# Three waits for the state-space mixer's end moved three steps later, with half-weight steps for the memory rows' sums

## The reference, cut to what matters

```python
h = rms_norm(x, norm_mix_g)
u = h @ w_in
y_ssd  = ssd_mixer(u[..., :SSD_IN], ...)     # ends in a grouped RMS norm
y_rwkv = rwkv7_mixer(u[..., SSD_IN:], ...)   # first uf = u + (u_prev - u) * mu
...
m = rms_norm(mem, norm_mem_g)                # 256 memory rows x 2048
k, v = m @ wk, m @ wv
```

## Time and profile before

| | before |
|---|---|
| median of three runs | 3058.83 us (3057.3 to 3061.13) |
| profiled execution | 3055.73 us, of which the span from first to last instruction is 3053.9 us |
| TensorE busy | 2975.5 us, 97% of the span |
| VectorE / ScalarE / GpSimd busy | 2074.0 / 1412.6 / 241.1 us |
| mean granted TensorE clock | 0.994 |
| chunks 33 to 39 of `in_rwkv` on TensorE | 294.29 to 316.17 us |
| longest TensorE idle time of the stage | 3.11 us |

### The profile page before, as it was taken

The page is one execution under the profiler, slowest core; times in us unless marked ns, Lnnn a source line. Parts: engine busy times, 40 slices in busy tenths (PEclk is TensorE's granted clock), DMA queues, the critical chain, the costliest instruction groups (busy, mean ns, idle before and its releaser), DMA issues.

```text
span 3053.9 us, 52430 instructions
## 1 busy us (share of the span) xinstructions
PE 2975.5 (97%) x21994; PEld 2632.0 (86%) x21994; DVE 2074.0 (68%) x2869; ACT 1412.6 (46%) x1977; POOL 241.1 (8%) x201
## 2 busy tenths in 40 slices
PE   8999999999999999999999999999989999999998
PEld 7899988887888888888888899888878888888887
DVE  6486864645656787888888985555677666666666
ACT  5343542534444563544445454444336445444453
POOL 1100321110100200000000310010010000000002
PEclk9999999999999999999999999999999999999999
DMA  7555566766645669888888877755345565665664
GB/s 250 166 167 156 158 222 206 225 196 227 209 138 159 214 198 280 274 277 277 273 279 277 271 234 225 221 151 170 109 131 162 183 187 178 202 187 184 180 186 132
DMA packets 527580, 619.94 MB, mean 203 GB/s; under 512 B 19450, under 2 KB 443541, under 8 KB 525984
## 3 DMA queue, kind: packets, MB, share of 16 engines
q1 hardware_dynamic: 518672, 586.31, 62.2%
q0 software_dynamic: 3344, 23.78, 2.2%
q10 hardware_dynamic: 5328, 6.49, 0.6%
HBM read 608.12 MB, written 8.39 MB: 202 GB/s over the span
## 4 chain that ended last, share of the span: by engine, by line
PE 90%; DVE 5%; issue 3%; ACT 1%; DMA 0%; POOL 0%; ACTq 0%; POOLq 0%; DVEq 0%; SPq 0%
PE psum L605 37%; PE psum L606 19%; PE psum L574 6%; PE psum L576 6%; PE psum L577 6%; PE psum L639 2%; PE psum L641 2%; PE psum L642 2%; DVE wlo L531 1%; PE psum L1851 1%; PE psum L706 1%; DVE cacc L1118 1%; PE psum L2563 1%; PE psum L2082 0%; PE psum L2304 0%
## 5 line engine op out<-in xcount | busy, mean ns | idle before, releaser
L524 ACT ACTIVATE whi<-wraw 128x1024 fp32r<-128x1024 f32 (+1 forms) x948 | 978.6, 1034 | 1001.2 <-PE psum L606 692.7
L531 DVE TENSOR_TENSOR wlo<-wraw,whi 128x1024 fp32r<-128x1024 f32 (+1 forms) x948 | 1151.2, 1230 | 244.6 <-ACT whi L524 244.1
L605 PE MATMUL psum<-g,whi 128*128 128x512 f32 x2816 | 996.1, 396 | 11.0 <-DVE g L2603 4.1
L605 PE MATMUL psum<-h,whi 128*128 128x512 f32 x2240 | 790.7, 395 | 2.3 <-DVE wlo L531 1.3
L606 PE MATMUL psum<-g,wlo 128*128 128x256 f32 x2816 | 787.0, 279 | 0.0
L605 PEld LDWEIGHTS psum<-g,whi 128*128 128x128 f32 x2816 | 529.0, 188 | 139.9 <-issue 8.4
L606 PE MATMUL psum<-h,wlo 128*128 128x256 f32 x2240 | 634.1, 283 | 0.0
L606 PEld LDWEIGHTS psum<-g,wlo 128*128 128x128 f32 x2816 | 529.2, 188 | 0.5
L605 PEld LDWEIGHTS psum<-h,whi 128*128 128x128 f32 x2240 | 421.4, 188 | 100.3 <-DVE wlo L531 1.6
L606 PEld LDWEIGHTS psum<-h,wlo 128*128 128x128 f32 x2240 | 421.9, 188 | 0.1
L574 PE MATMUL psum<-h,whi 128*128 128x256 f32 x1040 | 304.0, 292 | 22.0 <-DVE h L958 13.7
(11 more groups left out here) (488 smaller groups left out, 3191.3 us busy)
## 6 DMA issues: line engine op xcount, KB each, us to landing
wraw<-in_ffn_w SPq DMA_DIRECT2D x256, 512.0 KB, 4.9
wraw<-in_w_in SPq DMA_DIRECT2D x204, 512.0 KB, 3.7
wraw<-in_ada_w SPq DMA_DIRECT2D x192, 512.0 KB, 4.2
wraw<-in_ffn_w_up SPq DMA_DIRECT2D x160, 512.0 KB, 3.6
wraw<-in_w_out SPq DMA_DIRECT2D x64, 512.0 KB, 3.7
wraw<-in_ffn_w_down SPq DMA_DIRECT2D x64, 512.0 KB, 4.5
wraw<-in_xattn_wk SPq DMA_DIRECT2D x32, 512.0 KB, 4.6
wraw<-in_xattn_wv SPq DMA_DIRECT2D x32, 512.0 KB, 4.9
```

Source lines behind the costliest of these rows:

```text
L524: e.activation(high(i), raw(i), ACT.Copy).then_inc(*hi.up(i))
L531: e.tensor_tensor(low(i), raw(i), high(i).bitcast(F32), SUB).then_inc(*lo.up(i))
L605: e.matmul(both_of(g, j), w_hi[:, kk, s:s + 128], X[:, k, :], start=k == 0, stop=False, skip_group_check=True)
```

## The change

On all three engines three empty steps, `idle(3)`, come between the mixer's own steps and the wait for its end. The steps of the memory rows' sums weigh 0.5 in place of 1: on TensorE and VectorE the 7 empty ones and the one with the work, on ScalarE all 8. Nothing is added or removed in what is computed, and GpSimd's program is as before.

```diff
-            side = Side(ssd_p(e), then(psum_of_ssd_read, e), sums_p(e, mem, TM2, True), idle(12))
+            side = Side(ssd_p(e), idle(3), then(psum_of_ssd_read, e), sums_p(e, mem, TM2, True, 0.5), idle(12))
...
-            side = Side(ssd_v(e), then(ssd.ended, e), sums_v(e, mem, RS2, RC2[:, :]), mixing_v(e, 0, 12))
+            side = Side(ssd_v(e), idle(3), then(ssd.ended, e), sums_v(e, mem, RS2, RC2[:, :], 0.5), mixing_v(e, 0, 12))
...
-            side = Side(ssd_a(e), then(ssd.ended, e), then(mem_landed, e), sums_a(e, mem, MX, TM2, RS2, RC2[:, :]), idle(12))
+            side = Side(ssd_a(e), idle(3), then(ssd.ended, e), then(mem_landed, e), sums_a(e, mem, MX, TM2, RS2, RC2[:, :], 0.5), idle(12))
```

## The result

The changed kernel takes 3063.53 us (median of 20 runs, 3058.5 to 3066.43). The kernel before, run beside it, takes 3057.54 us (20 runs). The ratio is 1.0020, with a 95% interval of 1.0014 to 1.0026: about 6.0 us slower, at the edge of what was forecast as no measurable change (2.3 us). The profiled execution took 3064.98 us, its span 3063.2 us.

The account below looks back on a forecast made before the run. TensorE bounds, VectorE second: minus 3.1 of hole and 1.7 of clock, plus 6.2 of new wait and 1.7 of clock, net 2.2, rounded to plus 2.3 us: 3061.1 us as a median, range 3056.5 to 3066.6.

Parts of the forecast that it names:

- The removed wait: TensorE's wait for the mixer's end at 291: 3.11 us of hole and 1.7 us of low clock go, gaining 4.8.
- Where the steps fall: TensorE waits for the mixer after chunk 35 instead of 32, and makes the memory sums after chunk 38 instead of 39.
- the new hole: TensorE ahead of the memory sums: it waits for GpSimd's last add from 308.3 to 314.5, 6.2 us.
- The chain of squares and adds: ScalarE's squares and GpSimd's adds alternate strictly ahead of the sums: 11.0 us taken, 12.5 the other measurement.
- VectorE as the second bound: Without clock loss, VectorE's low part for chunk 47 at 341.3 bounds: plus 1.1 us, 3059.9; chance 0.15.
- The clock term: TensorE behind the new 6.2 us wait: low clock costs 1.7 us, at least nothing, at most 3.4.
- The sum: TensorE reaches chunk 47 at 342.4 against 340.24, a net of 2.2 us later, kept to the end.
- Range and chances: Whole-kernel time 3056.5 to 3066.6 us; chances 0.87 for same, 0.08 for slower, 0.05 for faster.
- the worst case summed up: Squares and adds taking 12.5 us and a clock loss of 3.4 us: plus 5.5 us, 3064.3.
- The 0.08 for slower: Chance of slower by more than 0.2%: the old hole not being this wait (3065.9), or very slow adds.
- no case but one: The one case: adds of up to 3.31 us and a long low-clock stretch on TensorE, 3064.3 us; chance 0.15.

Follow-up runs that it names:

- tensor_wait_late: Kernel before, with only TensorE's wait for the mixer's end three steps later and the memory sums kept behind chunk 39: 3052.78 us, ratio 0.9988.
- before_filled: Kernel before, with 7 extra unused matmuls on TensorE ahead of its wait for the mixer's end: ratio 0.9987, stage 1.7 us shorter.
- filled: Changed kernel, with 14 extra unused matmuls on TensorE ahead of its wait for GpSimd's last add: 3057.28 us, ratio to before 0.9998.
- sums_39: Changed kernel, with sums' steps of 0.65 on TensorE and VectorE (ScalarE keeps 0.5), so the sums come behind chunk 39: ratio to before 1.0003.
- half_only: Kernel before, with half steps for the sums on three engines, mixer waits unmoved, idle(3) behind VectorE's reciprocal: 3066.27 us, ratio 1.0026.

## Why the prediction was right in kind and short in size

- **The removed wait, 4.8 us:** right. `tensor_wait_late` shows 4.8, `before_filled` 1.7 for the clock alone.
- **Where the steps fall, and the new hole:** right. TensorE waits 6.04 us (6.2 forecast), the sums start at 314.57 (314.5).
- **The chain of squares and adds:** 10.6 us, a little under both bounds (11.0 and 12.5; 11.0 was taken), with adds of 2.34 to 2.48 us. Before, an add took 3.31 us beside VectorE's low parts. After, VectorE stood still for 17.01 us ahead of its reciprocal, and the two adds that began in that time took 2.34 us each. The Trainium skill (GPSIMD Engine Reference, 1. Specifications) says that GpSimd shares its SBUF interfaces with VectorE and contends with VectorE instructions that have two SBUF inputs, as L531 has. The trace agrees.
- **VectorE as the second bound at +1.1 us:** right where it came to bind, in `filled`. In the changed kernel the reciprocal was forecast for 318.6 and started at 322.26, because the sums ahead of it ran at the lower clock.
- **The clock term failed.** "For a hole of 6.2 us I take 1.7 us again; below nothing, above 3.4." It was 5.9: the sums took 7.0 us instead of 3.4, and chunk 39 took 326.8 - 321.6 = 5.2 instead of 2.85. The upper bound of 3.4 was itself too low. I took both numbers from stretches in which other matmuls followed the hole. What followed this one, L932 and L936, was in the trace, but I priced it by its duration at the full clock alone.
- **The sum again:** 2.2 + (5.9 - 1.7) = 6.4 us at TensorE; the stage grew by 5.9. Of the difference, 0.5 us, the start of the sums gives 0.2: the mixer's last L1204 starts 0.28 us later in this profile than in before's, and counted from there the sums start at 314.3, not at 314.5. The rest is tenths in the length of the sums and behind chunk 47.
- **Range and chances:** 3063.53 lies in the range, and in part by luck. The loss of 6.0 us is more than the worst case summed up, plus 5.5. The three runs of before that the forecast started from had a median 1.3 us above that of all 20, so the time is 2.4 us off the forecast of 3061.1 where the change is 3.7 us off. The kernel is slower by just 0.2%, and that is told from no change here: the interval reaches 1.8 us to each side. The 0.08 for slower was too little, because no case but one priced a longer low stretch.

## What to carry to other kernels

When a wait is moved to after its event, move the consumers behind it too: count, on every engine, in which iteration each step lands, and add up the chain across engines that must fit between. Here the three later steps alone were worth 4.9 us, and the half steps on top of them cost 10.8. A hole in TensorE's work costs its length plus the low clock behind it, and that second part depends on what runs next: behind the hole of 6.0 us it was 2.1 us with a full chunk first and 5.9 us with the sums first. If the hole can't be avoided, unused wide matmuls in it can keep the clock up: in `filled` they brought back 4.8 us of the stage. And take the gain from whole runs as well as from the stage, since a later hole can cost clock that the stage's measure doesn't see.

## What the runs showed of the hardware

I had not expected that matmuls issued without a gap could leave the granted clock low. Behind a hole of 6.0 us, with the two-column matmuls (128x128 by 128x2, 16 records) in the sums, the lower level lasted 13.6 to 13.7 us, in three profiles of three. With four matmuls of 256 columns (8 records) in their place it lasted 6.8 us, in one profile. In `sums_39` the two-column matmuls ran at the lower level behind a hole of 3.24 us, and the stretch lasted 10.2 us. In `half_only` the level had risen before they ran, and stayed up.

The Trainium skill (TensorE: Matmul & The Clock Gate, Why this matters for your kernels) warns of idle gaps between bursts of matmuls. The runs agree for the fall in this stage, with holes of 3.10 us and more followed by the lower level and holes of 0.55 and 0.44 us not; the length of the low stretch here came as much from what followed the gap. The hole of 1.79 us behind the stage was followed by the lower level in 5 profiles of 13; no run here shows what decides that.
